# A hybrid decoder step on one Trainium2 core: twenty slots for gathered cache pages, state rows turned behind the weight pair, three top-k rounds per convolution step

## The chip, the cores and the metric

One core of one Trainium2 chip runs the whole program. The metric is the time of one execution on the device in microseconds (us). The engines are named as the profile names them: PE is TensorE's matmul, DVE is VectorE, ACT is ScalarE, POOL is GpSimd, SP is the queue that issues most of the transfers.

## What is computed

One layer of a hybrid decoder on 512 prompt tokens and on 8 x 4 sampled tokens (544 columns in all). An RMS norm and one input projection of 2048 x 4688 give queries, keys and values, indexer queries and keys, and the input `u` of a convolution module.

```python
def conformer_conv(u, conv_prev, ...):
    a, gate = jnp.split(u, 2, axis=-1)
    g = a * jax.nn.sigmoid(gate)
    buf = jnp.concatenate([conv_prev, g], axis=1)      # 30 old rows, then the new ones
    y = depthwise_conv_31(buf)
    y = silu(layer_norm(y + conv_dw_bias, ...))
    return y, buf[:, -30:]                             # the new state
```

For each sampled token the indexer scores 2048 past keys and its own; the 256 largest are admissible, and attention runs over their cached keys and values, which lie in pages of 128 rows named by a page table. The prompt does the same with a top 128 of 512. Both parts are joined, go through an output projection, a SwiGLU layer of width 5632 and a final norm. The outputs are the tokens, the new keys, values and indexer keys, and the new convolution state.

## The kernel before

Activations lie with channels on partitions. A weight piece of 128 columns and 1024 rows is a *unit*. Each unit goes through a ring of four slots: SP loads it into `raw`, ACT rounds it to `whi` (L620), and DVE or POOL makes the rest `wlo = raw - whi` (L944, L549). PE then multiplies three products in the two halves of 272 columns, 48 matmuls per unit (L1501). Two units make a *tile* of 128 output columns in one half of PSUM, two tiles a *pair*. A tile may start once DVE has read the one that lay in its PSUM half (`s_ev`), and its weights are there (`s_lo`).

**The convolution stage** (about 229 to 490 us). Eight pairs P_U + c give the two halves of `u` for channel block c. DVE's `u_step(c)` reads the first half into `ga` and the second into `sg` (L1166), with the 21 taps that it does for block c - 1 between and behind them (L1133, into PSUM). Then `convolved(c - 1)` sums the sampled rows' products (L1141), adds the bias to them (L1143) and joins the sums (L1147, L1149); `gated(c)` copies the old state of the sampled rows (L1155), multiplies `ga` and the sigmoid into `gbuf` (L1157, L1158), and copies the rows that make the new state to `tg` (L1162, L1163). Last come two rounds of the sampled tokens' top-k (`topk_round`: MAX8, a copy of the eight found, MATCH_REPLACE8, a copy that spaces them). 32 such rounds are needed in all: 14 in this loop, the other 18 behind it as 4, 2, 2 and 10.

ACT makes the other 10 tap products (L738), and POOL adds them (L559), multiplies the sampled rows (L567) and makes all four `wlo` of the next pair (L549). Both start when `s_tg` says that `tg` is there. PE turns `tg` by a transpose (L1661, `new_state`), between the two tiles of the next pair:

```python
            with pe.Fori(1, CT) as i:
                tile(P_U + i, 0)
                new_state(i - 1)
                tile(P_U + i, 1)
```

**The norm of the convolution** (490 to 565 us). PE sums `y` with ones (L1678), DVE makes the mean, POOL subtracts it (L597) and then makes the weights of pair P_Q + 3 (`lows(P_Q + 2)`); ACT squares, PE sums (L1685), ACT takes the root. DVE, behind the last ten top-k rounds, takes the reciprocal `rl` (L1297), on which POOL multiplies `y` (L601, eight times) and only then makes the weights of pair P_K (`lows(P_Q + 3)`).

**Sampled attention** (682 to 780 us). Two groups of four sequences. Each group reads 16 chunks of key pages and 16 of value pages, a chunk being 4 pages of 128 KB; `n` counts the chunks from 0 to 63 (keys 0 to 15, values 16 to 31, keys 32 to 47, values 48 to 63). PE turns a key chunk in 8 transposes (L1759), ACT and DVE copy it out (L831, L1372), PE makes scores of four chunks (L1779); after the softmax it multiplies four value chunks at a time (L1813). `page_chunks` runs on SP and on POOL, each issuing two of a chunk's four pages (L406). Page numbers are read into registers by `value_load` (L387), 32 per queue and group: the first 32 ahead of all, the second 32 at n = 32. Sixteen slots hold chunks: 12 in the weights' rings (`ring_pages`), 4 of their own (`own_pages`), and the last four chunks have `late_pages`, which are free once the prompt's queries are used up. A slot is filled again when `s_chunk`, twice the number of chunks that PE has used, allows it:

```python
                if SLOTS <= n < 48:
                    eng.wait_ge(s_chunk, 2 * (n - SLOTS + 1))
                elif 48 <= n < 60:
                    eng.wait_ge(s_chunk, 2 * (n - 12 + 1))
```

Behind its chunks SP loads the four units of the output projection's first pair. PE's first unit of it follows the last value chunk. From there to the end PE works through the output projection and the feed-forward layer, 1800 us of weights.

## Time and profile before

| | us |
|---|---|
| median of 3 runs | 2596.65 |
| lowest, highest | 2593.91, 2597.6 |
| the profiled execution's own time | 2592.49 |
| its span, first to last instruction | 2590.8 |
| PE busy | 2488.7 (96%) |
| DVE busy | 1204.9 (47%) |
| ACT busy | 832.6 (32%) |
| POOL busy | 400.8 (15%) |

All durations come from the profiled execution, whose own time is 2592.49 us; 1.69 us of it lie around the span. Times of an instruction are counted from the span's start. In a timeline, the part in brackets is how long the engine had been idle before, and what ended it.
### The profile page before, as it was taken

To read this page: it belongs to the slowest core of one execution; us is meant where nothing else is said; L and a number is where in the kernel's file an instruction comes from. 1 tells how busy PE (TensorE), PEld (TensorE's weight loads), DVE (VectorE), ACT (ScalarE), POOL (GpSimd) and SP (SyncE) were. 2 spreads that over 40 slices of the span, in tenths; PEclk is the share of its full clock that TensorE was granted. 3 is DMA by queue.
4 is the path that set the end of the run, shared out by engine and by line. 5 is a ranking of instruction groups with operands and counts; after the bars stand their busy time and mean duration, and the time that the engine had idled before them with its cause. 6 is when DMAs were issued, how large, how long until landed. Compare 5 with 4: busy or idle time off the path is not lost.

```text
span 2590.8 us, 49958 instructions
## 1 busy us (share of the span) xinstructions
PE 2488.7 (96%) x19410; PEld 2401.0 (93%) x19412; DVE 1204.9 (47%) x1792; ACT 832.6 (32%) x1076; POOL 400.8 (15%) x438
## 2 busy tenths in 40 slices
PE   6989999988979999999999999999999999999998
PEld 6957998977649999999999999999999999999998
DVE  6578999896523335233333332333333333333354
ACT  5144344233522224333223333222333222222233
POOL 2314798742450000000000000000000000000000
PEclk9999999999989999999999999999999999999999
DMA  7404232223584342332233232233322223333222
GB/s 240 118 15 117 73 81 81 71 65 104 175 279 122 106 132 81 89 89 72 78 94 103 84 89 82 72 89 105 89 85 83 72 86 105 88 89 89 65 86 97
DMA packets 424724, 255.01 MB, mean 98 GB/s; under 512 B 19979, under 2 KB 413443, under 8 KB 423968
## 3 DMA queue, kind: packets, MB, share of 16 engines
q1 hardware_dynamic: 412864, 224.91, 30.0%
...
q14 instruction: 29, 0.24, 0.0%
...
## 4 chain that ended last, share of the span: by engine, by line
PE 83%; DVE 7%; issue 4%; DMA 2%; POOL 1%; ACT 1%; SPq 1%; DVEq 0%; ACTq 0%; POOLq 0%
PE ps L1501 77%; DVE ps L1133 1%; DVE scP L1059 1%; PE ps L1759 1%; PE ps L1738 1%; PE ps L1720 1%; PE ps L1612 1%; SPq L406 1%; SPq L387 1%; DMA xN<-in_x_prompt 1%; DMA own_pages<-in_cache_k 1%; POOL wlo L549 0%; POOL y L597 0%; ACT whi L620 0%; PE ps L1728 0%
## 5 line engine op out<-in xcount | busy, mean ns | idle before, releaser
L944 DVE TENSOR_TENSOR wlo<-raw,whi 128x1024 fp32r<-128x1024 f32 (+1 forms) x358 | 437.6, 1223 | 1121.8 <-ACT whi L620 1120.8
L1501 PE MATMUL ps<-xhi,whi 128*128 128x272 f32 (+1 forms) x4512 | 938.3, 289 | 21.6 <-POOL wlo L549 9.8
L1501 PE MATMUL ps<-xhi,wlo 128*128 128x272 f32 (+1 forms) x4512 | 936.5, 289 | 0.0
L1501 PE MATMUL ps<-xlo,whi 128*128 128x272 f32 (+1 forms) x4512 | 933.2, 288 | 0.0
L620 ACT CAST whi<-raw 128x1024 fp32r<-128x1024 f32 (+1 forms) x410 | 428.9, 1047 | 1208.6 <-PE ps L1501 1128.3
L1501 PEld LDWEIGHTS ps<-xhi,whi 128*128 128x128 f32 (+1 forms) x4512 | 711.4, 189 | 24.6 <-issue 14.8
L1501 PEld LDWEIGHTS ps<-xlo,whi 128*128 128x128 f32 (+1 forms) x4512 | 711.4, 189 | 0.0
L1501 PEld LDWEIGHTS ps<-xhi,wlo 128*128 128x128 f32 (+1 forms) x4512 | 706.6, 189 | 0.0
L1501 PE MATMUL ps<-hidh,whi 128*128 128x272 f32 x1408 | 291.1, 288 | 4.6 <-DVE hidl L1440 4.6
L1501 PE MATMUL ps<-hidl,whi 128*128 128x272 f32 x1408 | 290.7, 287 | 0.0
L1501 PE MATMUL ps<-hidh,wlo 128*128 128x272 f32 x1408 | 290.5, 287 | 0.0
L1501 PEld LDWEIGHTS ps<-hidh,whi 128*128 128x128 f32 x1408 | 219.1, 188 | 5.5 <-issue 5.5
L1501 PEld LDWEIGHTS ps<-hidl,whi 128*128 128x128 f32 x1408 | 219.2, 188 | 0.0
L1501 PEld LDWEIGHTS ps<-hidh,wlo 128*128 128x128 f32 x1408 | 219.2, 188 | 0.0
L549 POOL TENSOR_TENSOR wlo<-raw,whi 128x1024 fp32r<-128x1024 f32 x52 | 125.8, 2425 | 48.7 <-ACT whi L620 48.7
L1133 DVE SCALAR_TENSOR_TENSOR ps<-gbuf,cw,ps 128x512 f32<-128x512 f32 x152 | 101.5, 749 | 0.0
L559 POOL TENSOR_TENSOR y<-y,tap 128x512 f32<-128x512 f32 x72 | 94.0, 1306 | 3.5
L738 ACT ACTIVATE tap<-gbuf,cw 128x512 f32<-128x512 f32 x72 | 52.0, 722 | 78.4 <-POOL y L559 78.4
L899 ACT CAST hidh<-ut 128x544 f32 x44 | 28.5, 647 | 128.6 <-DVE ut L1438 128.6
L1440 DVE TENSOR_TENSOR hidl<-ut,hidh 128x544 f32 x44 | 31.9, 726 | 40.7 <-ACT hidh L899 40.7
L352 POOL DMA_DIRECT2D idxN<-in_cache_idx_k x64 | 34.2, 535 | 63.0 <-issue 63.0
L895 ACT ACTIVATE gt<-gt 128x544 f32<-128x544 f32 x44 | 29.0, 659 | 42.9 <-DVE gt L1446 42.9
...
## 6 DMA issues: line engine op xcount, KB each, us to landing
...
```

What stands on the lines that cost most here:

```text
L352: eng.dma_start(idxN[:, b % IB, bass.ds(g, 1), :].rearrange("p a d -> p (a d)"), ic[bass.ds(pg, 1), :, :].rearrange("a s d -> (a s) d")).t ...
L387: return [[eng.value_load(page[0:1, p + k:p + k + 1], min_val=0, max_val=NPOOL - 1) for k in range(k0, k1)] for p in at0]
L549: nc.gpsimd.tensor_tensor(wlo[:, u.slot, :, :], raw[:, u.slot, :, :], whi[:, u.slot, :, :].bitcast(F32), ALU.subtract).then_inc(s_lo, 1)
L559: nc.gpsimd.tensor_tensor(y2[:, :], y2[:, :], tap[(k - 1) % 2][:, :], ALU.add).then_inc(s_add, 1)
L620: nc.scalar.copy(whi[:, u.slot, :, 0:cols], raw[:, u.slot, :, 0:cols]).then_inc(s_hi, 1)
L738: nc.scalar.activation(dst, gbuf[:, ND + k:ND + k + SEQ], ACT.Copy, scale=cw[:, bass.ds(c, 1), ND + k]).then_inc(s_tap, 1)
L895: nc.scalar.activation(gt[:, :], gt[:, :], ACT.Silu).then_inc(s_silu, 1)
L899: nc.scalar.copy(tile_of(hidh, j), halves(ut[:, :])).then_inc(s_hh, 1)
L944: ve.tensor_tensor(wlo[:, u.slot, :, 0:cols], raw[:, u.slot, :, 0:cols], whi[:, u.slot, :, 0:cols].bitcast(F32), ALU.subtract).then_inc(s_ ...
L1133: ve.scalar_tensor_tensor(dst, gbuf[:, k:k + SEQ], wk, dst, ALU.mult, ALU.add).then_inc(s_conv, 1)
L1440: ve.tensor_tensor(tile_of(hidl, j), halves(ut[:, :]), tile_of(hidh, j).bitcast(F32), ALU.subtract).then_inc(s_hid, 1)
L1501: ins = te.matmul(ps[0:cols, 2 * slot + half, 0:HALF], w[:, u.slot, t, 0:cols], x[:, k0 + t, HALF * half:HALF * half + HALF], start=(hf == ...
```

## The change

1. PE's loop runs a whole pair and then turns the state rows; the same for P_Q.
2. The copies to `tg` and the copy of the old state go from DVE to ACT (`gated_rows`, `old_state`), with two new semaphores `s_gst` and `s_gnew`. `s_tg` is now raised by ACT. DVE's loop no longer counts on its chain semaphore.
3. The bias of the sampled rows is added once, for all eight blocks, behind the loop.
4. Three top-k rounds per step of the loop: 21 in it, 11 behind it as 4, 2, 2 and 3.
5. Sixteen slots and four late ones become twenty slots that are used in turn, `turn_pages` lying where `late_pages` lay; chunks are issued in order; PE waits for two chunks at a time. Of the second group's 32 page numbers per queue, 16 are read before chunk 16 is issued and 16 between chunks 24 and 31.
6. SP loads the first two units of the output projection right behind the chunks, the other two when the last chunk is used; ACT rounds the latter two behind the last attention output.

```diff
@@ page slots
-SLOTS, RSLOTS = 16, 12
+SLOTS, RSLOTS, OSLOTS = 20, 12, 16
+PAIRS = SLOTS // 2
-        own_pages = at("own_pages", [P, SLOTS - RSLOTS, 4, 256], F32, R0)
-        late_pages = at("late_pages", [P, 4, 4, 256], F32, S0)
+        own_pages = at("own_pages", [P, OSLOTS - RSLOTS, 4, 256], F32, R0)
+        turn_pages = at("turn_pages", [P, SLOTS - OSLOTS, 4, 256], F32, S0)
@@ page_slot
-            if n >= 60:
-                return late_pages[:, n - 60, :, :]
-            s = n % SLOTS if n < 48 else n - 44
+            s = n % SLOTS if n < 62 else n - 58
+            if s >= OSLOTS:
+                return turn_pages[:, s - OSLOTS, :, :]
@@ page_chunks
             eng.wait_ge(s_page, 16)
-            numbers = page_numbers(eng, 0, k0, k1)
+            numbers = [[page_numbers(eng, 0, m, k0, k1) for m in range(16)], []]
             eng.wait_ge(s_mm, 2 * M_OUT)
-            for n in list(range(48)) + list(range(60, 64)) + list(range(48, 60)):
+            for n in range(64):
                 g, v = n // 32, n // 16 % 2
-                if n == 32:
-                    numbers = page_numbers(eng, 1, k0, k1)
+                if n == 16:
+                    numbers[1] = [page_numbers(eng, 1, m, k0, k1) for m in range(8)]
                 if n == RSLOTS:
                     eng.wait_ge(s_mix, CT)
-                if SLOTS <= n < 48:
-                    eng.wait_ge(s_chunk, 2 * (n - SLOTS + 1))
-                elif 48 <= n < 60:
-                    eng.wait_ge(s_chunk, 2 * (n - 12 + 1))
+                if n >= SLOTS:
+                    eng.wait_ge(s_chunk, 2 * ((n if n < 62 else n + 2) - SLOTS + 1))
+                elif n == OSLOTS:
+                    eng.wait_ge(s_chunk, 1)
                 for k in range(k0, k1):
                     eng.dma_start(page_slot(n)[:, k, :],
-                                  (kc, vc)[v][bass.ds(numbers[n % 16][k - k0], 1), :, :].rearrange("a s d -> (a s) d")
-                                  ).then_inc(landed[n % SLOTS] if n < 60 else late, 16)
+                                  (kc, vc)[v][bass.ds(numbers[g][n % 16][k - k0], 1), :, :].rearrange("a s d -> (a s) d")
+                                  ).then_inc(landed[n // 2 % PAIRS], 16)
+                if 24 <= n < 32:
+                    numbers[1].append(page_numbers(eng, 1, n % 16, k0, k1))
@@ SP
-            sp.wait_ge(s_chunk, 2 * 36)
             for q in range(4):
+                if q == 2:
+                    sp.wait_ge(s_chunk, 128)
                 load(Unit(P_OUT, q), col(w_out, P * (q // 2), (1 - q, q % 2)[q // 2]))
@@ GpSimd, sampled_products
+                pool.wait_ge(s_gst, c + 1)
                 pool.wait_ge(s_tg, c + 1)
                 if not (isinstance(c, int) and c == 0):
-                    pool.wait_ge(s_ssum, 2 * c)
+                    pool.wait_ge(s_ssum, c)
@@ ScalarE; both are called behind state_rows(i - 1), and behind the first sigmoid_gate
+            def old_state(c):
+                if not (isinstance(c, int) and c == 0):
+                    act.wait_ge(s_smul, T * c)
+                nc.scalar.copy(gs[:, :, 0:CK - 1], stT[:, bass.ds(c, 1), :].rearrange("p a (b s) -> p (a b) s", b=B)
+                               ).then_inc(s_gst, 1)
+
+            def gated_rows(c):
+                act.wait_ge(s_gnew, c + 1)
+                nc.scalar.copy(tg[:, 0:CK - 1], gbuf[:, SEQ:SEQ + CK - 1])
+                nc.scalar.copy(tg[:, CK - 1:CK - 1 + NS].rearrange("p (b t) -> p b t", b=B), gs[:, :, CK - 1:]
+                               ).then_inc(s_tg, 1)
@@ ScalarE, sampled attention
                 if g == 1:
-                    act.wait_ge(s_chunk, 2 * 52)
-                    hi4(P_V)
+                    act.wait_ge(s_chunk, 2 * 48)
+                    for q in range(2):
+                        hi(Unit(P_V, 4 + q))
...
+            for q in range(2, 4):
+                hi(Unit(P_V, 4 + q))
@@ VectorE, convolved
                 ve.reduce_sum(ys, tapS[:, :, :, :].rearrange("p b t k -> p (b t) k"), AX.X).then_inc(s_ssum, 1)
-                dve.wait_ge(s_ssum, 2 * c + 1)
-                ve.tensor_scalar(ys, ys, vec[:, bass.ds(32 + c, 1)], None, ALU.add).then_inc(s_ssum, 1)
@@ VectorE, gated
                 if not (isinstance(c, int) and c == 0):
                     dve.wait_ge(s_conv, CN * c)
-                ve.tensor_copy(gs[:, :, 0:CK - 1], stT[:, bass.ds(c, 1), :].rearrange("p a (b s) -> p (a b) s", b=B))
+                    dve.wait_ge(s_tg, c)
                 dve.wait_ge(s_sg, c + 1)
                 ve.tensor_tensor(gbuf[:, CK - 1:CK - 1 + SEQ], ga[:, 0:SEQ], sg[:, 0:SEQ], ALU.mult)
-                ch.link(ve.tensor_tensor(gs[:, :, CK - 1:], ga[:, SEQ:].rearrange("p (b t) -> p b t", b=B),
-                                         sg[:, SEQ:].rearrange("p (b t) -> p b t", b=B), ALU.mult))
                 if not (isinstance(c, int) and c == 0):
-                    dve.wait_ge(s_tt, c)
-                ve.tensor_copy(tg[:, 0:CK - 1], gbuf[:, SEQ:SEQ + CK - 1])
-                ve.tensor_copy(tg[:, CK - 1:CK - 1 + NS].rearrange("p (b t) -> p b t", b=B), gs[:, :, CK - 1:]).then_inc(s_tg, 1)
+                    dve.wait_ge(s_smul, T * c)
+                ve.tensor_tensor(gs[:, :, CK - 1:], ga[:, SEQ:].rearrange("p (b t) -> p b t", b=B),
+                                 sg[:, SEQ:].rearrange("p (b t) -> p b t", b=B), ALU.mult).then_inc(s_gnew, 1)
@@ VectorE, u_step and what follows the loop
-                for k in range(2):
-                    topk_round(2 * c - 2 + k)
+                for k in range(3):
+                    topk_round(3 * c - 3 + k)
...
-            R1 = 2 * CT - 2
+            R1 = 3 * CT - 3
...
             convolved(CT - 1)
+            dve.wait_ge(s_ssum, CT)
+            ve.tensor_tensor(y[:, :, SEQ:NT], y[:, :, SEQ:NT], vec[:, 32:40].unsqueeze(2).to_broadcast([P, CT, NS]),
+                             ALU.add).then_inc(s_ssum, 1)
@@ TensorE
             with pe.Fori(1, CT) as i:
-                tile(P_U + i, 0)
+                pair(P_U + i)
                 new_state(i - 1)
-                tile(P_U + i, 1)
-            tile(P_Q, 0)
+            pair(P_Q)
             new_state(CT - 1)
-            tile(P_Q, 1)
...
+            def pages_landed(n):
+
+                pe.wait_ge(s_pg[n // 2 % PAIRS], 32 * SPP * (n // SLOTS + 1))
+                pe.wait_ge(s_pgp[n // 2 % PAIRS], 32 * (4 - SPP) * (n // SLOTS + 1))
@@ TensorE, keys(q); the value chunks call pages_landed(n0) and pages_landed(n0 + 2)
-                pe.wait_ge(s_pg[n % SLOTS], 16 * SPP * (n // SLOTS + 1))
-                pe.wait_ge(s_pgp[n % SLOTS], 16 * (4 - SPP) * (n // SLOTS + 1))
+                if n % 2 == 0:
+                    pages_landed(n)
```

On DVE, in the convolution loop, between the last sum and the first top-k round; before (`y` is the convolution's output, `m` and `tops` belong to the top-k, REGISTER_ALU and ISA are register work ahead of an instruction):

```order
L1149 TENSOR_TENSOR y<-ps,y 128x512
L1154 REGISTER_ALU
L1155 ISA
L1155 COPY gbuf<-stT 128x8x30
L1156 REGISTER_ALU
L1157 TENSOR_TENSOR gbuf<-ga,sg 128x512
L1158 TENSOR_TENSOR gbuf<-ga,sg 128x8x4
L104 REGISTER_ALU
L1162 COPY tg<-gbuf 128x30
L1163 COPY tg<-gbuf 128x32
L1175 MAX m_153<-scS 128x8
```

and now:

```order
L1170 TENSOR_TENSOR y<-ps,y 128x512
L1175 REGISTER_ALU
L1177 REGISTER_ALU
L1178 TENSOR_TENSOR gbuf<-ga,sg 128x512
L1180 REGISTER_ALU
L1181 TENSOR_TENSOR gbuf<-ga,sg 128x8x4
L1194 MAX m_153<-scS 128x8
L1195 ISA
L1196 ISA
L1196 COPY tops<-m_153 128x8
```

Three copies are gone; the top-k follows the second product directly. On PE, in the same loop, at the transpose of the state rows; before:

```order
L1501 MATMUL ps<-xhi,wlo 128x272 x2
L1660 REGISTER_ALU
L1661 MATMUL ps<-ident,tg 128x128
L1511 REGISTER_ALU
L1495 REGISTER_ALU
L1501 MATMUL ps<-xhi,whi 128x272 x2
```

and now:

```order
L1523 MATMUL ps<-xhi,wlo 128x272 x2
L1682 REGISTER_ALU
L1683 MATMUL ps<-ident,tg 128x128
L1686 REGISTER_ALU
L1686 COMPARE_AND_BRANCH
L1523 MATMUL ps<-xhi,whi 128x272 x2
```

The transpose stood behind a pair's first tile and stands behind its second, at the loop's end. On SP, in the sampled attention, where the second group's page numbers are read (TENSOR_LOAD and two ISA rows are one number); before:

```order
L406 DMA own_pages<-in_cache_k 128x256
L406 DMA ring_pages<-in_cache_v 128x256 x24
L406 DMA own_pages<-in_cache_v 128x256 x8
L387 TENSOR_LOAD page
L387 ISA x2
```

and now:

```order
L388 TENSOR_LOAD page
L388 ISA x2
L406 DMA turn_pages<-in_cache_v 128x256 x8
L406 DMA ring_pages<-in_cache_v 128x256 x10
L388 TENSOR_LOAD page
L388 ISA x2
L388 TENSOR_LOAD page
L388 ISA x2
```

The numbers stood as one block of 32 behind all value chunks of the first group; 16 now stand ahead of these, and two behind each of chunks 24 to 31.

## Rows read from the trace of the kernel before

**Rows 1.** The page: by engine, the chain that ended last

```profile
PE 83%; DVE 7%; issue 4%; DMA 2%; POOL 1%; ACT 1%; SPq 1%; DVEq 0%; ACTq 0%; POOLq 0%
```

**Rows 2.** Waits of PE, whole span: us in total, times, longest

```profile
PE ps L1661 <- DVE tg L1163: 12.9, 7, 2.5
```

**Rows 3.** Source line 1661, PE: min/median/max ns, first and last start

```profile
L1661 PE MATMUL ps<-ident,tg x8: 270/324/470, 265.7 to 451.2; 128*128 128x128 f32 x8
```

**Rows 4.** Windows: us, busy and count of PE, PEld, DVE, ACT, POOL; clock, DMA share, GB/s

```profile
562.60:571.60 9.00, 8.92 (x51) 8.96 (x52) 8.84 (x10) 0.04 (x1) 7.48 (x3) 0.68 0.70 182
571.60:577.60 6.00, 6.00 (x50) 6.00 (x50) 5.83 (x11) 1.04 (x2) 2.60 (x1) 1.00 0.28 80
```

**Rows 5.** Timeline of DVE, 398 to 428 us: start, us, instruction

```profile
398.65 0.72 DVE L1175 MAX8 m<-scS 128x8 f32<-128x544 f32 x1
...
401.38 0.31 DVE L1177 COPY tops<-m 128x8 f32 x1
...
402.81 0.72 DVE L1166 TENSOR_TENSOR ga<-ps,rstd 128x544 f32<-128x544 f32 x1 [0.24 <-issue]
...
411.42 0.72 DVE L1166 TENSOR_TENSOR sg<-ps,rstd 128x544 f32<-128x544 f32 x1 [1.24 <-PE ps L1501]
...
420.52 2.47 DVE L1143 TENSOR_SCALAR y<-y,vec  x1
...
424.66 0.69 DVE L1157 TENSOR_TENSOR gbuf<-ga,sg 128x512 f32<-128x512 f32 x1
```

**Rows 6.** Timeline of PE, 560 to 563 us

```profile
562.68 0.57 PE L1501 MATMUL ps<-xhi,whi 128*128 128x272 f32 x1 [9.79 <-POOL wlo L549]
```

**Rows 7.** Timeline of POOL, 448 to 625 us

```profile
477.50 4.76 POOL L549 TENSOR_TENSOR wlo<-raw,whi 128x1024 fp32r<-128x1024 f32 x2
...
548.61 11.44 POOL L601 TENSOR_TENSOR y<-y,rl 128x544 f32<-128x544 f32 x8 [25.19 <-DVE rl L1297]
```

**Rows 8.** Timeline of DVE, 448 to 625 us

```profile
478.48 3.82 DVE L1177 COPY tops<-m 128x8 f32 x1
...
544.98 3.55 DVE L1297 RECIPROCAL rl<-rl 128x544 f32<-128x544 f32 x1
```

**Rows 9.** Timeline of PE, 675 to 805 us

```profile
681.72 0.41 PE L1770 MATMUL ps<-biasS,rowsel 32*128 32x512 bf16 x5 [1.49 <-DVE xlo L1358]
...
719.07 0.63 PE L1818 MATMUL ps<-vN,pST 32*32 32x256 f32 x8
...
775.65 1.93 PE L1813 MATMUL ps<-own_pages,pST 128*32 128x256 f32 x32 [0.86 <-DMA own_pages<-in_cache_v]
...
779.80 0.52 PE L1501 MATMUL ps<-xhi,whi 128*128 128x272 f32 x2
```

**Rows 10.** Windows of the sampled attention, columns as in rows 4

```profile
710.00:723.00 13.00, 9.73 (x151) 5.91 (x149) 0.68 (x4) 3.31 (x12) 0.00 (x0) 0.96 0.01 4
723.00:779.80 56.80, 41.80 (x361) 27.79 (x361) 15.41 (x26) 16.60 (x33) 34.11 (x64) 0.83 1.04 330
```

**Rows 11.** Timeline of SP's queue, 700 to 745 us

```profile
701.24 3.69 SPq L406 DMA_DIRECT2D own_pages<-in_cache_v  x8
723.06 12.56 SPq L406 DMA_DIRECT2D ring_pages<-in_cache_k  x24
```

**Rows 12.** Timeline of POOL, 398 to 428 us

```profile
399.01 2.65 POOL L567 TENSOR_TENSOR tapS<-gbuf,cw 128x248 f32<-128x248 f32 x4 [3.06 <-DVE tg L1163]
...
402.87 2.40 POOL L549 TENSOR_TENSOR wlo<-raw,whi 128x1024 fp32r<-128x1024 f32 x1
405.24 4.01 POOL L559 TENSOR_TENSOR y<-y,tap 128x512 f32<-128x512 f32 x3
...
420.56 2.38 POOL L549 TENSOR_TENSOR wlo<-raw,whi 128x1024 fp32r<-128x1024 f32 x1
```

**Rows 13.** Source line 1143, DVE: min/median/max ns

```profile
L1143 DVE TENSOR_SCALAR y<-y,vec x8: 241/806/2473, 289.2 to 476.1; - x7, 128x32 f32<-128x32 f32 x1
```

**Rows 14.** Timeline of ACT, 755 to 815 us

```profile
777.10 1.04 ACT L620 CAST whi<-raw 128x1024 fp32r<-128x1024 f32 x1 [10.12 <-issue]
```

38 lines of the change are left out of this document (18 added, 20 removed).

## The prediction

> **What bounds the kernel now.** I read the chain that ended last first. PE is 83% of it [rows 1], and the matmuls of the weights are most of that; they are not touched. So only a stage in which PE waits can give time, or one in which its clock is low. Three places lie inside the change.
>
> First the convolution loop. PE waits 12.9 us in seven places for `tg` [rows 2], and its eight transposes of `tg` lie between 265.7 and 451.2 us [rows 3]: a step of 26.5 us, while four units keep PE busy for 24.1 (some 50 matmuls take 6.00 us at full clock [rows 4], a unit has 48). The loop closes over two engines: PE waits for `tg`, turns it, runs one tile (12 us), DVE reads `sg` from that tile, does its last 11 taps, the sums and the gating, and only then makes `tg`. On DVE that stretch goes from 411.42, where DVE had waited 1.24 us for PE, past 424.66 [rows 5].
>
> Second the norm of the convolution. At 562.68 us PE has waited 9.79 us for POOL's `wlo` [rows 6]. POOL makes it behind the multiplication by `rl`, which waited 25.19 us for DVE [rows 7]; and DVE takes the reciprocal at 544.98 [rows 8], behind ten top-k rounds.
>
> Third the sampled attention. Group 0 takes PE from 681.72 to 719.70 us, 38.0 us; group 1 ends at 779.80 [rows 9]. Between 710 and 723 us the transfers move 4 GB/s, then 330 GB/s to the end [rows 10]: SP finishes the chunks of group 0 at 704.93 and issues the next at 723.06, since it reads 32 page numbers in between [rows 11], 0.57 us each. From there group 1 runs at the pace of the stream (at 775.65 PE still waits for pages [rows 9]), at a granted clock of 0.83 [rows 10].
>
> **The loop, part by part.** With the transpose behind the pair and ACT copying, PE is out of the circle. What is next? *PE alone* needs 24.1 and a transpose, 24.4 us. *POOL* works from 399.01 to 422.94 [rows 12], 23.9 us, and then needs the next `tg`: DVE's two products (0.8), ACT's copies (0.3 to 0.4, estimated from the small copies' 0.2) and two hand-overs (0.4). The product L1157 has both inputs in SBUF and can't start before POOL's last `wlo` ends, as I argue below; so POOL's step is 25.5 us. *DVE alone*: from 402.81 to 424.66 it takes 21.85 us [rows 5], of which go the wait for PE (1.24), L1143 (2.4 until the next could start) and the copy L1155 (0.2): 18.0. The products are 0.7, and three rounds 6.1 (two took 402.81 - 398.65 = 4.16 [rows 5]). That is 24.8 us.
>
> So 25.5 us would be the step if nothing got in the way. But L1143 shows what can: on 32 columns it takes 0.24 us at best and 2.47 at worst [rows 13]. At 420.52 it starts 0.04 us ahead of a POOL `wlo` of 2.38 us [rows 12] and ends with it. The copy of a top-k round does the same: 3.82 us at 478.48 [rows 8], under two `wlo` from 477.50 to 482.26 [rows 7]. The second round's copy at 401.38 slips between two POOL instructions (0.31 us). The third round that is added has such a copy. POOL's products begin some 0.8 us behind the first MAX8, since ACT's copies lie between; its first `wlo` runs from 3.9 to 6.3 us behind their begin [rows 12]. The rounds' copies come 0.87 us into rounds of 1.9: the first meets the first product (0.66 us) and waits 0.5, and the third comes 4.4 us behind POOL's begin, inside the `wlo`, and waits 1.8. DVE then needs 24.8 + 2.2 = **27.0 us**: a lock wait takes the place of the one in L1143, now in every step. Lower bound 25.5 (the copy gets in first), upper 28.3 (a 1.3 us tap sum goes ahead of it too). I take 27.0, since the arrival lies 0.5 us inside.
>
> The Trainium skill, page "SBUF — State Buffer", section "Who interferes with whom", says that copies and tensor_scalar in a two-port mode, and instructions with two SBUF inputs, contend with GpSimd for a shared pair of ports, and that whoever issues first holds it for its whole instruction; ScalarE never waits. By this rule the third copy is a cost of the change, as forecast; without it the step would be 25.5 us and the sum 10.8 us less. By the same rule a copy should go between two GpSimd instructions; the 3.82 us copy outlasted the first of two, so the trace does not wholly agree.
>
> Seven steps: the first, in which DVE is late with the prompt's rounds, loses the removed copies and bias, 0.5 us; six go from 26.5 to 27.0: +3.0. The old-state copy on ACT costs nothing, ACT waits for `sg` and for POOL most of the loop. Behind the loop DVE has one more round (+1.9) and one more lock wait (+1.8) before it frees PSUM for pair P_Q + 2; of its four rounds' lock waits (3.6 us in that one copy) I expect 3 to go, as the pair is no longer split and POOL's `wlo` lie elsewhere. The bias once is below 0.5 us, inside that. **Loop and exit: +2.5 + 0.7 = +3.2 us.**
>
> **The norm.** Seven rounds fewer at 2.1 us are 14.6: the reciprocal begins at 530.4 instead of 544.98, POOL's eight products end at 545.4 (3.55 + 11.44 later), its first `wlo` at 547.8. PE needs it at 552.9. So the wait goes with 5 us to spare: -9.8. Behind the idle stretch 51 matmuls took 8.92 us at a granted clock of 0.68; at 1.00 they take 6.1 [rows 4]: -2.8, the half-speed level (1.2 GHz) that followed the wait. **Together -12.6.** DVE has nothing late behind it: it sorts while PE runs P_Q + 3 and P_K.
>
> **The pages.** SP can start at 683.2, one chunk behind PE's begin. Chunks 16 to 31 cost 16 x 1.1 us (24 issues took 12.56 us [rows 11]) and 16 of the numbers 16 x 0.57: done at 710. The other 16 are read under the prompt's attention, where SP has nothing to do; POOL's queue is alike. Chunk 32 takes a slot that chunk 12 left, free long before. So group 1's stream starts 13.1 us earlier; 32 chunks are 16.8 MB, 50.8 us at 330 GB/s, and the last page lands at 762.5 instead of 775.6. PE without a wait would be at the end of group 1 at 721.4 + 38.0 = 759.4, so the stream still decides: four chunks' products and the tail, 2.6 us, end at 765.1. Then the first weight: its cast began 1.5 us behind the last page (777.10 [rows 14]), it takes 1.04, the rest about as long, hand-overs 0.4: 766.5, so PE waits 1.4 us for what was hidden before. 779.80 - 766.5 = **-13.3**. The last two units, loaded at about 765, are needed 13 us later and take some 9: hidden. Bounds: -20 (PE's own pace and weights in time), -8 (the stream half as much earlier). Waiting for chunks in twos costs nothing where the stream is ahead.
>
> The Trainium skill, page "SBUF — State Buffer", section "Summary: rules for kernel authors", gives 358 GB/s from HBM; by that the stream would take 46.9 us and the sum would be 2 to 3 us less. The rows show 330, and I keep it.
>
> **Sum.** +3.2 - 12.6 - 13.3 = -22.7: 2592.49 becomes 2569.8 for the profiled execution. That one lies 4.2 us below the median of the three runs, 2596.65; on the median's footing the forecast is **2574 us**.
>
> **Rivals.**
> A, *the copy gets in first*: steps of 25.5 us, 6 x 1.5 less, and 1.8 less at the exit: 2563 us. For it: the second copy slipped in, and the margin is 0.5 us on estimated ACT times. Against: L1143 lost by 0.04 us.
> B, *the stream gains half*: the numbers between the chunks and PE's fast release leave SP's queue behind, so that group 1 starts 5 us earlier only: +8: 2582. Against: SP's own count above.
> C, *the wait in the norm stays* because DVE or POOL is late from the loop: +12.6: 2587. Against: 5 us to spare.
> D, *slower*: POOL keeps the ports through back-to-back instructions, as under the 3.82 us copy. The third copy then waits for three tap sums (4.01) and the next `wlo` (2.40) as well [rows 12], 6.4 us in each of six steps: +38.5, 2612 us. It decides from about 4 us per step. Against: the copy at 401.38 slipped in, and tap sums wait for ACT and leave gaps.
> E, the edits cancel (B, C and longer steps together): 2594 to 2600.
>
> **How the numbers follow.** A measurement of this kernel tells about 0.2% (5 us) from no change. Chances: forecast 0.48 (2568 to 2580 alone), A 0.30, B 0.12, C 0.03, D 0.05, E 0.02. Faster 0.93, same 0.02, slower 0.05. The range, 2557 to 2584, takes in A with a little more from the pages, and B.
>
> **What would show it.** PE's transposes of `tg` without a wait, but 27.0 us apart, with the third `tops` copy near 2 us and the first near 0.7; 25.5 apart would be A. No wait of PE at the start of P_K. Transfers above 200 GB/s between 700 and 720 us of the old time, first key page of group 1 by 713; PE's waits for pages only at the last values, then 1 to 2 us for `wlo`. Wrong would be a PE that waits inside the keys of group 1, or steps above 29 us.

## The result, and the profile after

The changed kernel takes 2569.11 us in the median of four runs (2566.93 to 2575.52), against 2596.37 us (2593.91 to 2597.6, four runs) for the kernel before: a ratio of 0.990, 95% interval [0.9885, 0.9916]. The profiled execution took 2568.09 us, 24.4 us less than that of before. It is 1% faster, inside the range that was forecast (2557 to 2584) and 5 us below the forecast itself (2574).

| profiled execution, us | before | after |
|---|---|---|
| its own time | 2592.49 | 2568.09 |
| span | 2590.8 | 2566.4 |
| PE busy | 2488.7 | 2486.8 |
| DVE busy | 1204.9 | 1196.4 |
| POOL busy | 400.8 | 399.8 |

In the page's chain of what ended last PE has 84% where it had 83 [rows 1]:

```profile
PE 84%; DVE 8%; issue 4%; ACT 1%; DMA 1%; DVEq 1%; SPq 0%; ACTq 0%
```

Line numbers from here on are those of the kernel whose profile is shown. In the changed kernel L1683 is the transpose of `tg` (L1661 before), L1523 PE's matmuls, L552 POOL's `wlo`, L571 its products and L562 its tap sums, L1196 the copy of a top-k round, L1185 the read of `ga` or `sg`, L1305 the bias of all eight blocks, L1038 the rotary step that frees PSUM.

**A common zero for the stages.** The start of a program differs from run to run: over all the profiles of this study DVE reads the first `ga` at between 239.83 and 246.97 us, ahead of every changed instruction. So I count stages from that instruction. DVE's timeline of before (start, duration, instruction, idle time before it and its releaser):

```profile
241.88 0.72 DVE L1166 TENSOR_TENSOR ga<-ps,rstd 128x544 f32<-128x544 f32 x1 [1.80 <-PE ps L1501]
```

And in the changed kernel:

```profile
240.34 0.72 DVE L1185 TENSOR_TENSOR ga<-ps,rstd 128x544 f32<-128x544 f32 x1 [1.80 <-PE ps L1523]
```

1.5 of the 24.4 us are therefore no work of the change. The other 22.9 are split as follows, each line from first instruction to first instruction (differences are taken before rounding):

| stage, us | before | after | difference | forecast |
|---|---|---|---|---|
| first `ga` to P_Q + 2 | 252.7 | 254.6 | +1.8 | +3.2 |
| P_Q + 2 to the first page of the sampled attention | 187.5 | 174.8 | -12.6 | -12.6 |
| first page to P_OUT | 97.7 | 83.4 | -14.3 | -13.3 |
| P_OUT to the end | 1811.0 | 1813.3 | +2.3 | 0 |
| sum | | | -22.8 | -22.7 |

**The loop.** PE turns `tg` eight times without a wait (line 1683 by itself), where it had waited 12.9 us [rows 2, 3]. Line 1683 (min, median and max ns, first and last start):

```profile
L1683 PE MATMUL ps<-ident,tg x8: 270/271/273, 276.2 to 457.8; 128*128 128x128 f32 x8
```

PE's waits there are now for PSUM, freed by DVE (us in total, times, longest):

```profile
PE ps L1523 <- DVE ga L1185: 8.2, 5, 2.2
...
PE ps L1523 <- DVE rt L1038: 3.6, 2, 2.0
```

POOL's timeline gives the step, 423.93 - 397.25 = 26.68 us, where 27.0 was forecast. Over the six steps it is 26.65 on average; before it was 26.48, four steps of 27.0 and two of 25.4 (from the products at 292.59 to those at 451.44).

```profile
397.25 2.68 POOL L571 TENSOR_TENSOR tapS<-gbuf,cw 128x248 f32<-128x248 f32 x4 [2.76 <-ACT tg L738]
...
423.93 2.65 POOL L571 TENSOR_TENSOR tapS<-gbuf,cw 128x248 f32<-128x248 f32 x4 [2.74 <-ACT tg L738]
...
427.76 2.41 POOL L552 TENSOR_TENSOR wlo<-raw,whi 128x1024 fp32r<-128x1024 f32 x1
430.11 1.29 POOL L562 TENSOR_TENSOR y<-y,tap 128x512 f32<-128x512 f32 x1
```

DVE's timeline of the same step shows why. The first copy of a round takes 0.63 us, the second 0.30, the third 1.94: it starts half a microsecond into POOL's `wlo` of 427.76 and ends with it.

```profile
424.02 0.63 DVE L1196 COPY tops<-m 128x8 f32 x1 [0.15 <-DVE m L1194]
...
426.31 0.30 DVE L1196 COPY tops<-m 128x8 f32 x1
...
428.26 1.94 DVE L1196 COPY tops<-m 128x8 f32 x1
```

**Behind the loop.** DVE adds the bias at 481.35 us, under the last of three `wlo` of POOL, and ends 0.3 us behind it. The pair P_Q + 2 waits 1.61 us for DVE (DVE, POOL, then PE). In the kernel before PE came to this pair without a wait, and its sums of `y` began 245.6 us behind the first `ga` (487.48), now 245.5 (485.79): the +1.8 us of the stage are this wait.

```profile
481.35 2.49 DVE L1305 TENSOR_TENSOR y<-y,vec 128x256 f32<-128x256 f32 x1
```

The same stretch of POOL:

```profile
476.43 7.12 POOL L552 TENSOR_TENSOR wlo<-raw,whi 128x1024 fp32r<-128x1024 f32 x3
```

The same stretch of PE:

```profile
494.89 0.52 PE L1523 MATMUL ps<-xhi,whi 128*128 128x272 f32 x2 [1.61 <-DVE rt L1038]
```

**The norm.** DVE's reciprocal is at 530.56 and no longer at 544.98 [rows 8]; POOL's products by `rl` still wait, 10.32 us and not 25.19 [rows 7], and PE no longer waits at P_K [rows 6] (DVE, then the window in which P_K begins, with a granted clock of 1.00 where 0.68 followed the wait [rows 4]):

```profile
530.56 3.55 DVE L1319 RECIPROCAL rl<-rl 128x544 f32<-128x544 f32 x1
...
552.00:562.00 10.00, 10.00 (x82) 10.00 (x81) 9.66 (x22) 8.79 (x11) 3.14 (x2) 1.00 0.49 141
```

The same stretch of POOL:

```profile
534.19 11.09 POOL L605 TENSOR_TENSOR y<-y,rl 128x544 f32<-128x544 f32 x8 [10.32 <-DVE rl L1319]
545.24 7.26 POOL L552 TENSOR_TENSOR wlo<-raw,whi 128x1024 fp32r<-128x1024 f32 x3
```

**The pages.** SP issues the first chunk of the second group at 696.22, with the `own` pages of chunk 32, 26.5 us behind PE's first page (669.70); before it was 41.0 us behind (723.06 - 682.06 [rows 11]). The stream no longer stops between the groups: 351 and 348 GB/s where 4 had been [rows 10] (the row of SP's queue, then windows, then PE).

```profile
696.22 3.94 SPq L406 DMA_DIRECT2D own_pages<-in_cache_k  x8
```

The windows (us, busy and count of PE, PEld, DVE, ACT, POOL; clock, DMA share, GB/s):

```profile
700.00:712.00 12.00, 10.71 (x154) 6.96 (x147) 1.05 (x3) 1.78 (x7) 9.38 (x18) 0.90 1.05 351
712.00:730.00 18.00, 18.00 (x143) 12.55 (x142) 8.81 (x14) 6.80 (x12) 14.46 (x28) 0.97 1.07 348
```

The same stretch of PE:

```profile
743.07 1.93 PE L1833 MATMUL ps<-own_pages,pST 128*32 128x256 f32 x32 [0.61 <-DMA own_pages<-in_cache_v]
746.08 1.93 PE L1833 MATMUL ps<-turn_pages,pST 128*32 128x256 f32 x32 [1.08 <-DMA turn_pages<-in_cache_v]
749.10 1.93 PE L1833 MATMUL ps<-ring_pages,pST 128*32 128x256 f32 x32 [1.09 <-DMA ring_pages<-in_cache_v]
...
753.12 0.49 PE L1523 MATMUL ps<-xhi,whi 128*128 128x272 f32 x2 [1.53 <-DVE wlo L967]
...
761.80 0.39 PE L1523 MATMUL ps<-xhi,whi 128*128 128x272 f32 x1 [0.69 <-DVE xlo L1412]
```

PE waits for pages only at the last three values, about 1 us each, then 1.53 us for the first `wlo` of P_OUT. The row of 753.12 stands for -14.3. The next one shows part of it going back: that unit took until 761.80, 8.68 us, and before 7.21 (779.80 to 787.01); the granted clock over it was 0.80, before 1.00 (windows of after, then of before):

```profile
753.12:761.80 8.68, 7.98 (x51) 7.75 (x51) 1.55 (x3) 0.97 (x4) 0.00 (x0) 0.80 0.43 119
...
779.80:787.01 7.21, 6.52 (x55) 6.28 (x51) 1.64 (x4) 2.88 (x6) 0.00 (x0) 1.00 0.11 29
```

From there to the end the two differ by 0.8 us, which is inside what runs show: it is 1803.8 to 1806.8 us over all the profiles of the study, at identical work.

### The profile page after: what moved, and what is told of

The parts are those of the page before. It is cut to its first block, busy times and chain, and to the rows that moved or that the text cites. A ratio compares the mean times of both kernels' runs of the same rounds, so it can differ in the third digit from the quotient of the medians.

```text
span 2566.4 us, 49915 instructions
## 1 busy us (share of the span) xinstructions
PE 2486.8 (97%) x19412; PEld 2405.7 (94%) x19412; DVE 1196.4 (47%) x1761; ACT 837.3 (33%) x1100; POOL 399.8 (16%) x438
## 4 chain that ended last, share of the span: by engine, by line
PE 84%; DVE 8%; issue 4%; ACT 1%; DMA 1%; DVEq 1%; SPq 0%; ACTq 0%
PE ps L1523 77%; DVE ps L1156 2%; PE ps L1784 1%; DVE scP L1082 1%; DVE scS L1197 1%; PE ps L1758 1%; DVE m L1194 1%; PE ps L1804 1%; PE ps L1740 1%; PE ps L1634 1%; DMA xN<-in_x_prompt 1%; ACT whi L624 0%; PE ps L1833 0%; PE ps L1748 0%; PE ps L1891 0%
## 5 line engine op out<-in xcount | busy, mean ns | idle before, releaser
L1523 PE MATMUL ps<-xhi,whi 128*128 128x272 f32 (+1 forms) x4512 | 939.3, 289 | 23.2 <-DVE ga L1185 8.2
L1523 PE MATMUL ps<-xhi,wlo 128*128 128x272 f32 (+1 forms) x4512 | 938.0, 289 | 0.0
L1523 PE MATMUL ps<-xlo,whi 128*128 128x272 f32 (+1 forms) x4512 | 934.7, 289 | 0.0
L1523 PEld LDWEIGHTS ps<-xhi,whi 128*128 128x128 f32 (+1 forms) x4512 | 712.5, 189 | 27.5 <-issue 13.4
L1523 PEld LDWEIGHTS ps<-xlo,whi 128*128 128x128 f32 (+1 forms) x4512 | 712.6, 189 | 0.0
L1523 PEld LDWEIGHTS ps<-xhi,wlo 128*128 128x128 f32 (+1 forms) x4512 | 708.0, 190 | 0.0
L1523 PE MATMUL ps<-hidh,whi 128*128 128x272 f32 x1408 | 291.2, 288 | 4.6 <-DVE hidl L1462 4.6
L1523 PE MATMUL ps<-hidl,whi 128*128 128x272 f32 x1408 | 290.7, 287 | 0.0
L1523 PE MATMUL ps<-hidh,wlo 128*128 128x272 f32 x1408 | 290.6, 287 | 0.0
L1523 PEld LDWEIGHTS ps<-hidh,whi 128*128 128x128 f32 x1408 | 219.1, 188 | 5.5 <-issue 5.5
L1523 PEld LDWEIGHTS ps<-hidl,whi 128*128 128x128 f32 x1408 | 219.2, 188 | 0.0
L1523 PEld LDWEIGHTS ps<-hidh,wlo 128*128 128x128 f32 x1408 | 219.2, 188 | 0.0
L552 POOL TENSOR_TENSOR wlo<-raw,whi 128x1024 fp32r<-128x1024 f32 x52 | 125.5, 2419 | 50.2 <-ACT whi L624 50.2
L562 POOL TENSOR_TENSOR y<-y,tap 128x512 f32<-128x512 f32 x72 | 93.5, 1299 | 3.5
L1462 DVE TENSOR_TENSOR hidl<-ut,hidh 128x544 f32 x44 | 31.9, 726 | 40.7 <-ACT hidh L922 40.7
```

What stands on the lines that cost most here:

```text
L552: nc.gpsimd.tensor_tensor(wlo[:, u.slot, :, :], raw[:, u.slot, :, :], whi[:, u.slot, :, :].bitcast(F32), ALU.subtract).then_inc(s_lo, 1)
L562: nc.gpsimd.tensor_tensor(y2[:, :], y2[:, :], tap[(k - 1) % 2][:, :], ALU.add).then_inc(s_add, 1)
L1462: ve.tensor_tensor(tile_of(hidl, j), halves(ut[:, :]), tile_of(hidh, j).bitcast(F32), ALU.subtract).then_inc(s_hid, 1)
L1523: ins = te.matmul(ps[0:cols, 2 * slot + half, 0:HALF], w[:, u.slot, t, 0:cols], x[:, k0 + t, HALF * half:HALF * half + HALF], start=(hf == ...
```

## The experiments

Each kernel was timed beside the one before on the same chip, in five rounds; ratios are to the kernel before, with the 95% interval. Stages are counted from the first `ga`, as above. A profile is one execution and can lie off the median of its kernel: those of `act_bias` (2571.99 us, median 2563.05) and `numbers_block` (2585.28, median 2579.75) lie the furthest.

### One part alone: the pages (pages_only)

The kernel before, with of the change only the slots, their numbers and what hangs on them:

```diff
+SLOTS, RSLOTS, OSLOTS = 20, 12, 16
+                if n == 16:
+                    numbers[1] = [page_numbers(eng, 1, m, k0, k1) for m in range(8)]
...
+                if 24 <= n < 32:
+                    numbers[1].append(page_numbers(eng, 1, n % 16, k0, k1))
```

> The kernel before with the page part of the change alone (20 slots in pairs, second group's numbers read early, the last weights loaded in two halves). Theory 1, the parts add: the loop and the norm stay as before (PE's step 26.5 us, wait for wlo in the norm 9.8), the sampled attention ends 14.3 us earlier, 0.8 us is given back behind it: 13.5 us less, 0.9948 of before. Rival, the stage gained because PE came into it with another clock or in another phase of the stream: less than 10 us, above 0.996.

Measured: 2577.65 us, 0.9953 [0.9935, 0.9972], where 0.9948 was expected. From the first page to P_OUT it takes 83.5 us, as the changed kernel does, and from the first `ga` to the first page 437.8, where before has 440.2 and the changed kernel 429.4 (in this profile three of the six loop steps and not two are short ones of 25.4 us). So the page part works by itself, and the rival (less than 10 us, above 0.996) falls.

### The other part alone: the convolution (conv_only)

The kernel before, with of the change only the order of PE, the copies, the bias and the rounds:

```diff
+                pair(P_U + i)
+                new_state(i - 1)
+                for k in range(3):
+                    topk_round(3 * c - 3 + k)
...
```

> The kernel before with the convolution part alone (transposes behind the pair, old state and gated rows copied by ScalarE, bias once, three rounds per step; pages as before; one semaphore fewer, as s_gst says nothing that s_tg doesn't). Theory 1, the parts add: steps of 26.7 us, the pair P_Q + 2 at the time of before, no wait for wlo in the norm, all later stages 12.4 us earlier: 0.9952 of before. Rival, both parts are needed for one gain: the two ratios leave out less than 20 of the 27 us together.

Measured: 2580.56 us, 0.9952 [0.9939, 0.9965], as expected. Steps of 26.58 us; the first page comes 428.9 us behind the first `ga` (before 440.2), and from there to P_OUT 98.4 (before 97.7). The two parts alone leave out 0.47% and 0.48%, together 24.7 us of some 2596; the whole change leaves out 1.0% (0.9% in its second timing). Within the intervals they add, and the rival (less than 20 us together) falls.

### Which of the two in the pages: numbers or slots (numbers_block)

```diff
-                if n == 16:
-                    numbers[1] = [page_numbers(eng, 1, m, k0, k1) for m in range(8)]
+                if n == 32:
+                    numbers[1] = [page_numbers(eng, 1, m, k0, k1) for m in range(16)]
-                if 24 <= n < 32:
-                    numbers[1].append(page_numbers(eng, 1, n % 16, k0, k1))
```

> The changed kernel (20 slots, pairs), but each queue reads all 16 x 2 numbers of the second group in one block at chunk 32, as before. Theory, the numbers between the groups were what left the DMA engines idle: SP ends chunk 31 near 687 and issues chunk 32 near 705 instead of 696.2, some 9 us of stream lost and moved to the end: P_OUT 8 to 9 us later, 0.9933 of before. Rival, the four more slots alone gave the gain, since SP then runs far enough ahead: 0.9905 or less. A third way, half of each: 0.992.

Measured: 2579.75 us, 0.9954 [0.994, 0.9969], slower still than the first theory's 0.9933; the rival (0.9905 or less) and the third way (0.992) fall. From first page to P_OUT it takes 95.0 us, against 97.7 before and 83.4 in the changed kernel: of the 14.3 us the place of the numbers gives 11.6, with the rest of the page part in place. The other 2.7 belong to all that is left of it together (the four slots, the order of the chunks, the waits in twos, the output projection's loads in halves); that was not taken apart, and the numbers moved without the slots were not run. SP's queue shows the 18 us in which it issues nothing, and PE waits at the first key page of the group (SP, then PE):

```profile
680.68 18.09 SPq L406 DMA_DIRECT2D ring_pages<-in_cache_v  x24
716.89 3.96 SPq L406 DMA_DIRECT2D own_pages<-in_cache_k  x8
```

The same stretch of PE:

```profile
723.19 5.54 PE L1782 MATMUL ps<-ident,own_pages 128*128 128x128 f32 x32 [7.26 <-DMA own_pages<-in_cache_k]
```

Chunk 32 goes out 40.7 us behind PE's first page (716.89 - 676.23); before it was 41.0. I had expected SP to be done with chunk 31 some 17 us behind PE's begin; it was 22.5. So the rest of the page part does not by itself bring the second group's first chunk forward (0.3 us).

### Two rounds per step (two_rounds)

```diff
-                for k in range(3):
-                    topk_round(3 * c - 3 + k)
+                for k in range(2):
+                    topk_round(2 * c - 2 + k)
```

> The changed kernel with two rounds per step as before, and seven more behind the loop. Theory 1: steps of 25.4 us (the third copy is gone), 7.5 us less, but the reciprocal comes 7 rounds (14.6 us) later than it does, so PE waits again for wlo in the norm, some 9 to 10 us at the start of P_K, and runs the tile behind it at a low clock (2.8 us): 2569 - 7.5 + 12.4 = 2574 us, 0.9914 of before. Rival, the step doesn't hang on the third copy: steps of 26.7, the norm's wait back, 2581 us or more. Rival, the rounds behind the loop were never what the norm waited for: 2561 us.

Measured: 2573.91 us, 0.9927 [0.9914, 0.994]: the first theory's 2574 us (its 0.9914 is the interval's end, since before was 4 us faster here), and both rivals fall. Steps are 25.29 us, and in PE's waits the norm's is back:

```profile
PE ps L1523 <- POOL wlo L552: 12.2, 5, 10.0
```

So the third round costs 1.36 us in each of six steps and takes a wait of 10.0 us, and the low clock behind it, out of the norm: P_Q + 2 to the first page is 187.3 us here and 174.8 in the changed kernel. One row was not expected. With DVE early, its bias instruction arrives 0.18 us ahead of four `wlo` of POOL, and is held until they have ended (DVE, then POOL; DVE 469.20 to 479.02, POOL to 478.72):

```profile
469.20 9.82 DVE L1305 TENSOR_TENSOR y<-y,vec 128x256 f32<-128x256 f32 x1
```

The same stretch of POOL:

```profile
468.18 0.62 POOL L590 DMA_DIRECT2D out_conv_prompt<-cout  x1
468.78 0.58 POOL L591 DMA_DIRECT2D out_conv_sample<-cout  x1
469.38 9.34 POOL L552 TENSOR_TENSOR wlo<-raw,whi 128x1024 fp32r<-128x1024 f32 x4
```

### The copies of a step to ScalarE (act_tops)

In the loop the MAX8 of round k writes `m8[:, k]`, and ScalarE copies all three:

```diff
-                ve.tensor_copy(tops[:, bass.ds(8 * r, 8)], m8[:, 0, :])
...
+            def found_tops(j):
+                act.wait_ge(s_topk, 6 * (KP_ // 8) + 6 * j - 1)
+                nc.scalar.copy(tops[:, bass.ds(24 * j - 24, 24)], m8[:, 0:3, :].rearrange("p a n -> p (a n)"))
```

> The changed kernel, with the three copies of a step's rounds to tops taken from VectorE: the three MAX8 of a step write three places of m8, and ScalarE copies all three to tops before its next sigmoid. Theory 1, the third copy's wait under GpSimd's wlo (1.93 us) with the first one's (0.63) is what makes a step 26.7 and not 25.4 us: steps of 25.4, held by GpSimd's 23.95 us of work and 1.5 of hand-over; six steps give 7.5 us, which stay to the end: 2561.5 us, 0.9866 of before. Rival 1, GpSimd's circle sets the step whatever VectorE does: 26.7, 2569 us. Rival 2, the wait moves to another two-input instruction of VectorE: steps between 26 and 26.7.

Measured: 2564.93 us, 0.9888 [0.9873, 0.9902], less gain than the 0.9866 expected. The loop does what the first theory says: steps of 25.29 us (25.4 expected, the rivals' 26 to 26.7 fall), ScalarE's copies taking 0.20 to 0.21. But behind the loop the bias instruction takes 7.47 us, and PE waits 4.35 before the sums of the norm, which then run slower (9.06 us for 7.50). The profile names no releaser for that wait, but the sums start 0.1 us behind the bias's end here (482.28 behind 482.17), as in the kernel with two rounds (479.12 behind 479.02). DVE, POOL, PE:

```profile
474.70 7.47 DVE L1317 TENSOR_TENSOR y<-y,vec 128x256 f32<-128x256 f32 x1
```

The same stretch of POOL:

```profile
472.52 9.36 POOL L552 TENSOR_TENSOR wlo<-raw,whi 128x1024 fp32r<-128x1024 f32 x4
```

The same stretch of PE:

```profile
482.28 9.06 PE L1710 MATMUL ps<-y,ones 128*128 128x272 f32 x32 [4.35 <-issue]
492.74 0.52 PE L1535 MATMUL ps<-xhi,whi 128*128 128x272 f32 x2 [1.40 <-DVE rt L1046]
```

P_Q + 2 comes 248.2 us behind the first `ga`, 6.4 earlier than in the changed kernel; 8.2 were gained in the loop.

### The bias to ScalarE (act_bias)

```diff
-            ve.tensor_tensor(y[:, :, SEQ:NT], y[:, :, SEQ:NT], vec[:, 32:40].unsqueeze(2).to_broadcast([P, CT, NS]),
-                             ALU.add).then_inc(s_ssum, 1)
+            def bias_rows(c):
+                act.wait_ge(s_ssum, c + 1)
+                ys = y[:, bass.ds(c, 1), SEQ:NT].rearrange("p a n -> p (a n)")
+                nc.scalar.activation(ys, ys, ACT.Identity, bias=vec[:, bass.ds(32 + c, 1)], scale=1.0).then_inc(s_yb, 1)
```

> As act_tops, and the bias of the sample rows is added by ScalarE, channel block by channel block in the loop; VectorE's one instruction for all of them behind the loop (7.47 us in act_tops, 9.82 in two_rounds, 2.49 in the changed kernel) is gone. Theory, the lock hits whichever two-port instruction of VectorE comes first while GpSimd works without a gap: the sums of PE no longer wait (4.35 us and 1.6 of low clock), but the first round's copy behind the loop now takes the wait, about 6 us, so P_Q + 2 comes only 1 us earlier than in act_tops: 0.988 of before. Rival, the long instruction was long because it reads and writes 256 columns of y, and a small copy slips in: the pair P_Q + 2 comes 6 us earlier, 0.9865.

Measured: 2563.05 us, 0.9892 [0.9875, 0.9909]. The theory's row is there: the wait has passed to the next copy, of eight columns, which takes 6.37 us and ends with the `wlo` series. The rival (the size of the instruction) falls. P_Q + 2 comes 247.0 us behind the first `ga`, 1.2 earlier than in the kernel with the copies alone on ScalarE. In this profile that isn't kept: PE now waits 4.58 us in one piece ahead of P_Q + 2, the granted clock over the 7.2 us behind it is 0.69, and the first page comes 425.6 us behind the first `ga`, where it was 422.9. The medians of the two kernels can't be told apart.

```profile
476.63 6.37 DVE L1213 COPY tops<-m 128x8 f32 x1
```

The same stretch of POOL:

```profile
473.60 9.36 POOL L552 TENSOR_TENSOR wlo<-raw,whi 128x1024 fp32r<-128x1024 f32 x4
```

### Nothing left for the lock behind the loop, twice (act_all, act_all2)

ScalarE's copy stands behind its casts of P_Q + 2; the last two lines are GpSimd's:

```diff
-            topk_sample(R1, 4)
+            for k in range(4):
+                topk_round(R1 + k, k)
...
+            nc.scalar.copy(tops[:, 24 * CT - 24:24 * CT + 8], m8[:, 0:4, :].rearrange("p a n -> p (a n)")).then_inc(s_tc, 1)
...
-                pool.wait_ge(s_tg, c + 1)
+                pool.wait_ge(s_gnew, c + 1)
```

> As act_bias, and ScalarE also copies the found values of the four rounds behind the loop, and GpSimd's products wait for s_gnew (the gated product) and no longer for s_tg (ScalarE's copies behind it). Theory: VectorE has no instruction behind the loop that the lock can hold, its four rounds take 7.6 us right behind the sums of the last block, P_Q + 2 starts when PE has ended the sums, some 6 us earlier than in act_bias; steps of 24.8 us instead of 25.3 give 3 us more: about 2555 us, 0.985 of before. Rival, something else holds P_Q + 2, such as PSUM or GpSimd's wlo: 0.987 or more.

Measured: 2567.06 us, 0.99 [0.9883, 0.9918]. This one missed by my own edit: ScalarE comes to the copy only at 510.76, behind casts that wait for PE, and DVE stood still for it:

```profile
511.17 0.73 DVE L1212 MAX8 m<-scS 128x8 f32<-128x544 f32 x1 [25.14 <-ACT tops L799]
```

The next kernel has the copy ahead of those casts, and no other difference.

> act_all with ScalarE's copy of the four rounds in front of the casts of P_Q + 2 and not behind them, where it made VectorE wait 25.14 us. Theory, the lock is the only thing between act_bias and this: P_Q + 2 starts 6 to 7 us earlier than in act_bias, counted from the first ga (act_bias 247.0 us, here 240.5), and the later stages keep it: 14 us less than the changed kernel, 2556 us, 0.986 of before. Rival, the norm's chain (mu, GpSimd, the rounds left, the reciprocal) becomes the bound and gives back half: 0.989.

Measured: 2553.88 us, 0.9851 [0.9834, 0.9868]: the fastest kernel of the study, and clear of the changed one (its interval begins at 0.9885). Steps are 24.92 us. P_Q + 2 starts at 480.47, 239.2 us behind the first `ga` and 7.7 earlier than with the bias alone moved; 3.0 of these are there by the loop's last products (the shorter steps, which come of GpSimd's earlier start and not of the lock), 4.7 come behind the loop. The first page of the sampled attention comes 15.5 us earlier than in the changed kernel, and PE shows no wait for POOL in the norm: the rival, a norm that gives back half, falls. PE's sums (7.57 us) wait 1.46:

```profile
473.27 7.57 PE L1718 MATMUL ps<-y,ones 128*128 128x272 f32 x32 [1.46 <-issue]
```

### Gaps in POOL's series (act_tops_gaps)

```diff
-            lows(P_Q + 1)
...
+            low(Unit(P_Q + 1, 4))
             pool.dma_start(o["conv_prompt"][0, 0], cout[0:CK - 1, :]).then_inc(s_cvo, 16)
+            low(Unit(P_Q + 1, 5))
...
+            low(Unit(P_Q + 1, 6))
+            low(Unit(P_Q + 1, 7))
```

> act_tops with the two stores that GpSimd issues behind the loop put between its wlo subtractions of P_Q + 1 (behind the first and the second) and no longer ahead of all four. Theory, VectorE's bias instruction waits for the next gap of GpSimd, of any length, not for the whole stage: it takes 0.3 to 2.6 us instead of 7.47, and what waits after it is a copy under the last two subtractions; PE's wait of 4.35 us ahead of the sums is gone or below 1; 3 to 5 us less than act_tops, 0.987 of before. Rival, the wait has another cause than back-to-back work (the stores themselves, or the size of the instruction): 7 us or more as before, 0.989.

Measured: 2563.29 us, 0.9884 [0.9869, 0.9899], not to be told from the 0.9888 without it, and the theory falls: DVE's bias takes 7.54 us, through the stretch of 0.60 us in which POOL only issues a transfer (it came 0.4 us behind the first issue). DVE, then POOL:

```profile
470.33 7.54 DVE L1320 TENSOR_TENSOR y<-y,vec 128x256 f32<-128x256 f32 x1
```

The same stretch of POOL:

```profile
469.95 2.41 POOL L552 TENSOR_TENSOR wlo<-raw,whi 128x1024 fp32r<-128x1024 f32 x1
472.29 0.60 POOL L593 DMA_DIRECT2D out_conv_sample<-cout  x1
472.92 4.67 POOL L552 TENSOR_TENSOR wlo<-raw,whi 128x1024 fp32r<-128x1024 f32 x2
```

PE's wait of 4.4 us stayed as well. This stretch in which POOL issues was no gap for DVE. POOL waiting itself was one: in the kernel with the bias once (below) DVE's instruction ends 0.3 us after two `wlo`, where POOL stands 0.59 us for ScalarE.

### The transposes back in the middle of the pair (split_pair)

```diff
-                pair(P_U + i)
-                new_state(i - 1)
+                tile(P_U + i, 0)
+                new_state(i - 1)
+                tile(P_U + i, 1)
```

> The changed kernel with the transpose of tg in the middle of a pair again, as before. Theory 1, PE's circle is 12.6 us from tg to sg and, without the bias and the three copies on VectorE, 12.5 us back to tg, 25.1 in all, below the 26.65 that VectorE with its third copy needs: the step stays 26.65, PE's waits go from ga back to tg, and the time is that of the changed kernel, 0.990 to 0.991. Rival, the circle through PE is what the order of before cost, and the third round lengthens it: steps of 28.4 us, 10 us more, 0.994.

Measured: 2570.13 us, 0.991 [0.9897, 0.9924]; steps of 26.64 us, and 513.3 us from first `ga` to P_OUT, where the changed kernel has 512.8. The rival (steps of 28.4 us, 0.994) falls: PE waits for `tg` again, seven times, and it costs nothing:

```profile
PE ps L1683 <- ACT tg L738: 10.1, 7, 2.1
```

The changed place of the transposes is not what pays for the third round. In a kernel with steps of 24.9 us it might be, since PE's circle was worked out at 25.1; that wasn't tried.

### The bias once, and nothing else (bias_once)

```diff
-                dve.wait_ge(s_ssum, 2 * c + 1)
-                ve.tensor_scalar(ys, ys, vec[:, bass.ds(32 + c, 1)], None, ALU.add).then_inc(s_ssum, 1)
+            ve.tensor_tensor(y[:, :, SEQ:NT], y[:, :, SEQ:NT], vec[:, 32:40].unsqueeze(2).to_broadcast([P, CT, NS]),
+                             ALU.add).then_inc(s_ssum, 1)
```

> The kernel before with the bias of the sample rows added once behind the loop and nothing else. Theory 1, four of its six steps are 27.0 and two 25.4 us because the small bias instruction sometimes starts under a wlo and waits 2.4 us: all steps become 25.4, 6 us less by the loop's end, of which the bias instruction behind the loop takes 3 to 4 back by its own wait under GpSimd: 2 to 3 us less in all, 0.999 of before. Rival 1, another two-port instruction of VectorE takes the wait: steps of 27.0, no gain, 1.001. Rival 2, the wait behind the loop is 7 to 10 us, as in act_tops and two_rounds: 1.001 with steps of 25.4.

Measured: 2590.8 us, 0.9983 [0.9974, 0.9992]. Five of the six steps are 25.3 to 25.4 us, the first 26.0; before, four were 27.0. So the small bias instruction that started 0.04 us ahead of a `wlo` [rows 5, 12] was the 1.6 us, as the first theory has it. P_OUT comes 533.1 us behind the first `ga`, 4.8 earlier than before, and the norm keeps its wait of 10.0 us. Both rivals (1.001) lie outside the interval. DVE's row behind the loop, and POOL's (480.03 is the subtraction that waited):

```profile
474.51 5.22 DVE L1284 TENSOR_TENSOR y<-y,vec 128x256 f32<-128x256 f32 x1
```

The same stretch of POOL:

```profile
474.69 4.75 POOL L549 TENSOR_TENSOR wlo<-raw,whi 128x1024 fp32r<-128x1024 f32 x2
480.03 2.39 POOL L549 TENSOR_TENSOR wlo<-raw,whi 128x1024 fp32r<-128x1024 f32 x1 [0.59 <-ACT whi L620]
```

### The changed kernel again (after_again)

> The changed kernel once more, beside the three others of this call: 0.990 of before, loop steps of 26.65 us.

Measured: 2568.88 us, 0.9913 [0.9897, 0.9929], steps of 26.65 us. First `ga` to P_OUT is 513.1 us here and 512.8 in the first profile, while the first `ga` itself lies at 244.67 and 240.34: the clock from the first `ga` repeats within a few tenths where the whole span moves by 5.6 us.

## Why the prediction was right, point by point

**The loop (forecast +2.5, measured +0.7).** The mechanism was right, the size of one term high. The first step gave back 0.5 us as forecast (34.14 to 33.64 us). The six others cost 1.07 us and not 3.0, since the step is 26.65 and not 27.0 us. The copies waited as forecast (1.94 us in all for the third where 1.8 was added to its 0.17, 0.63 for the first); the mis-sized term is DVE's step without any wait, 24.8 in the working and some 24.3 by this profile (26.65 less 1.8, 0.5 and 0.1): from `ga` to the first product DVE takes 17.8 us where 18.0 stood, and three rounds without their waits 5.9 where 6.1 stood. (The working added 2.2 for waits of 0.5 and 1.8; and its 24.1 us of PE for four units do not follow from the row beside it, which would give 23.0. Nothing hung on either.) POOL's circle, forecast as 25.5, is 25.29: both the kernel with the copies on ScalarE and the one with two rounds run at it, 1.36 us a step below the changed kernel.

**Behind the loop (forecast +0.7, measured +1.1).** The sum came near by luck of its parts. The bias once "below 0.5 us" took 2.49, since it came under the last of three back-to-back `wlo`; the four rounds' copies, of whose 3.6 us of waits three were to go, waited only 0.5 us in all (0.17, 0.17, 0.67 and 0.17 us). The lock's wait is one wait, and whichever instruction comes first pays it: five kernels have it on the bias (7.47, 9.82, 5.22 us), on a copy (6.37) and on nothing. This is the step the working was weakest at.

**The slower rival** priced such a wait at 6.4 us in each step and asked for POOL to keep the ports through back-to-back instructions. It does not in the loop, but in the series behind it DVE waited as if it did, and a faster loop brings DVE there earlier: 2.49 us at 481.35, 7.47 at 474.70, 9.82 at 469.20. So the kernel with steps 1.36 us shorter kept only 6.4 of the 8.2 us that it had by the end of the loop.

**The norm (forecast -12.6, measured -12.6).** Right in its place and size: the reciprocal at 530.56 (530.4 forecast), POOL's products by `rl` end at 545.3 (545.4), no wait of PE. The kernel with two rounds brings the wait of 10.0 us back. The low clock went with it: 1.00 from 552 to 562 us, where 0.68 followed the wait [rows 4].

**The pages (forecast -13.3, measured -14.3, then +2.3 behind).** SP's count was right within 1.4 us: chunk 32 leaves 26.5 us behind PE's first page, and the working had it at 710, 27.9 us behind (682.1). The forecast laid it all on the numbers that are read between the groups; the kernel with the numbers in one block gives them 11.6 of 14.3 us, and 2.7 to the rest of the page part, which I had given nothing. PE's wait for the first `wlo` was 1.53 (1.4 forecast). What was missed is that the unit behind that wait ran at a granted clock of 0.80 and took 1.5 us longer: the kind of cost that was charged to the norm's wait, and could have been charged here. What brings it on wasn't isolated, since three short waits for pages stand ahead of this one. It doesn't come each time: of the ten other profiles with the pages changed (the one with the numbers in one block among them), five show 8.68 or 8.69 us at 0.80 and five 7.15 to 7.20 at 1.00, four of these behind much the same wait. The rival in which the stream gains half (0.12) has no row for it.

The Trainium skill's figure for the HBM stream (page "SBUF — State Buffer", section "Summary: rules for kernel authors", 358 GB/s) would, as an estimate by the working's own numbers, have made it 3.9 us less (50.8 - 46.9) and not the 2 to 3 written there. The windows show 351 and 348 GB/s from 700 to 730 us and 335 from 730 to 750, all below the page's. The 330 of before is a mean over the whole group [rows 10], so this is no proof that the stream itself became faster.

**The level.** 2574 was made for a median that lies 4.2 us above the profiled time. In the runs after the change the profiled 2568.09 lies 1.0 below the median of 2569.11. Those 3 us are most of the miss on the median; the rest of it is the 1.5 us by which that run's first `ga` came earlier.
